# Strassen FFN kernel: late low parts, the down weight loads, the centre taps and one residual add change their places

## What is computed

```python
def conv_ffn(x, norm_g, w_up, conv_w, conv_b, w_down):      # w_up 1024 x 5632, w_down 2816 x 1024
    h = causal_depthwise_conv(rms_norm(x, norm_g) @ w_up, conv_w, conv_b)   # width 3
    g, u = jnp.split(h, 2, axis=-1)
    return (jax.nn.silu(g) * u) @ w_down

x = x + conv_ffn(x, ...)                                    # in both layers
z = rms_norm(x, norm_g) @ w_in                              # first step of layer 1's mixer
```

## Time and profile before

| | us |
|---|---|
| median of three runs | 2183.09 (2181.4 to 2183.55) |
| profiled execution | 2179.79 |
| its span, first to last instruction | 2178.0 |
| mean granted clock of TensorE | 0.991 |
| TensorE busy | 2117.4 |
| VectorE busy | 1419.3 |
| GpSimd busy | 1262.8 |
| ScalarE busy | 888.7 |

### The profile page before, as it was taken

How to read it: one execution, slowest core, us unless ns; L and a number is a source line. 1 busy time by engine, 2 the same in 40 slices (tenths; PEclk the granted TensorE clock), 3 DMA queues, 4 the chain that set the end, 5 groups by cost and what they waited for, 6 DMA issues and landing times. The chain is left out here.

```text
span 2178.0 us, 26915 instructions
## 1 busy us (share of the span) xinstructions
PE 2117.4 (97%) x10027; PEld 1741.1 (80%) x10027; DVE 1419.3 (65%) x1545; ACT 888.7 (41%) x1396; POOL 1262.8 (58%) x808
## 2 busy tenths in 40 slices
PE   9999999999999998998899999999999999999997
PEld 8777778878888787886788898888788788778876
DVE  7766777667777776565743344286777777765655
ACT  6555452544443433433344333434443344433331
POOL 2222117687778773688553333266877778745782
PEclk9999999999999999999999999999999999999999
DMA  6111003022232334343321021030222332333332
GB/s 204 58 49 40 34 17 139 21 87 87 92 131 91 113 107 182 108 134 108 131 88 49 30 72 54 30 136 29 78 81 94 116 116 87 119 145 135 139 130 87
DMA packets 57345, 204.19 MB, mean 94 GB/s; under 512 B 6848, under 2 KB 8960, under 8 KB 55168
## 3 DMA queue, kind: packets, MB, share of 16 engines
q1 hardware_dynamic: 47136, 163.22, 22.3%
q10 hardware_dynamic: 10080, 39.24, 4.9%
HBM read 151.81 MB, written 46.43 MB: 91 GB/s over the span
## 5 line engine op out<-in xcount | busy, mean ns | idle before, releaser
L1696 POOL TENSOR_TENSOR w_lo<-w_sum,w_hi 128x512 fp32r<-128x512 f32 x240 | 362.4, 1520 | 178.1 <-ACT w_hi L1690 178.1
L2318 POOL TENSOR_TENSOR w_hi<-w_raw,ones 128x1024 fp32r<-128x1024 f32 x54 | 106.3, 1969 | 496.1 <-PE pj L336 170.4
L1690 ACT ACTIVATE w_hi<-w_sum 128x512 fp32r<-128x512 f32 x240 | 145.3, 628 | 468.0 <-POOL w_sum L1711 194.7
L1696 POOL TENSOR_TENSOR w_lo<-w_raw,w_hi 128x512 fp32r<-128x512 f32 x180 | 240.5, 1344 | 90.4 <-ACT w_hi L1690 89.5
L1765 PE MATMUL pj<-t_hi,w_hi 128*128 128x512 f32 x520 | 205.5, 395 | 15.2 <-DVE ffn_v L1874 15.2
L1765 PE MATMUL pj<-t_lo,w_hi 128*128 128x512 f32 x520 | 203.7, 392 | 0.0
L1765 PE MATMUL pj<-t_hi,w_lo 128*128 128x512 f32 x520 | 203.5, 391 | 0.0
L1690 ACT ACTIVATE w_hi<-w_raw 128x512 fp32r<-128x512 f32 x180 | 111.6, 626 | 127.6 <-PE pj L1765 60.7
L1840 PE MATMUL dn<-pair,w_hi 128*128 128x512 f32 x512 | 158.2, 390 | 1.0 <-POOL w_lo L1696 0.9
L1840 PE MATMUL pj<-pair,w_hi 128*128 128x512 f32 x384 | 121.7, 399 | 18.2 <-POOL w_lo L1696 18.1
L2320 POOL TENSOR_TENSOR w_lo<-w_raw,w_hi 128x1024 fp32r<-128x1024 f32 x54 | 135.9, 2516 | 4.2
(11 more groups left out here) (421 smaller groups left out, 5449.5 us busy)
## 6 DMA issues: line engine op xcount, KB each, us to landing
w_raw<-weights SPq DMA_DIRECT2D x187, 512.0 KB, 3.9
gated_rows<-ffn_gated SPq DMA_DIRECT2D x72, 512.0 KB, 2.9
pair_stage<-gated_rows ACTq DMA_DIRECT2D x16, 1024.0 KB, 6.4
pair_stage<-gated_rows ACTq DMA_DIRECT2D x16, 512.0 KB, 4.5
x_first<-x_t SPq DMA_DIRECT2D x8, 512.0 KB, 7.4
res<-x_t SPq DMA_DIRECT2D x8, 512.0 KB, 6.5
pair_stage<-gated_rows ACTq DMA_DIRECT2D x16, 256.0 KB, 3.5
scratch<-res ACTq DMA_DIRECT2D x8, 512.0 KB, 2.7
```

Of the source, the lines that this page charges most:

```text
L1690: act.activation(f.cut(t, whi), f.source(j, name), ACT.Copy).then_inc(c_high, 1)
L1696: pool.tensor_tensor(f.cut(t, wlo), f.source(j, name), f.cut(t, whi).bitcast(F32), ALU.subtract).then_inc(c_ready, 1)
L2318: pool.tensor_tensor(whi[:, w, :], raw[:, r, :], ones[:, 0:1].to_broadcast([P, D]), ALU.mult).then_inc(w_high, 1)
```

## The change

Six places change, all in the order of work; no instruction is added or removed.

- DOWN_ORDER begins with chunk 20 (still in SBUF) and has chunk 0 second.
- In the last up tile VectorE makes the gated product of chunk 20 ahead of c11, and the first low part behind c11.
- `dve_gated_low` of the last two chunks moves from block 6 (ahead of the a22 and the s4 adds) to block 7 (behind u2, and behind the a11 add).
- SyncE issues the three weight loads of down ahead of the last pair's T transfers.
- On ScalarE `act_center(j - 1, 1)` stands ahead of the split of step 1, and `act_center(j, 0)` moves from behind the split of step 6 to ahead of that of step 4.
- `dve_layer1` goes add d, norm d - 1, for every d, where it had two adds and two norms, twice, and then add and norm in turn.

```diff
-DOWN_ORDER = (0, FC - 2, 1, 2, 3, FC - 1)
+DOWN_ORDER = (FC - 2, 0, 1, 2, 3, FC - 1)
...
             dve_block_add(dve, f, m, "u2", u, f.block_room("s2"))
+            if m == N_BLOCK - 1:
+                dve_gated_low(dve, f, DOWN_SIZES[0])
             dve_block_prod(dve, f, m, "s3")
...
             if m + 2 < N_PAIR:
                 dve_pair_low_half(dve, f, m + 2, 0)
-            elif m == N_BLOCK - 2:
-                dve_gated_low(dve, f, DOWN_SIZES[0])
             dve_block_prod(dve, f, m, "a22")
...
             if m + 2 < N_PAIR:
                 dve_pair_low_half(dve, f, m + 2, 1)
-            elif m == N_BLOCK - 2:
+            elif m == N_BLOCK - 1:
                 dve_gated_low(dve, f, DOWN_SIZES[0] + 1)
             dve_block_prod(dve, f, m, "s4")
...
             dve_c21(dve, f, j)
+            dve_gated(dve, f, j - 1)
+            dve_c11(dve, f, j)
             dve_gated_low(dve, f, 0)
-            dve_c11(dve, f, j)
-            dve_gated(dve, f, j - 1)
             dve_c12(dve, f, j)
...
                     if i == 1:
                         act_p1(act, f, j)
+                        if j > 1:
+                            act_center(act, f, j - 1, 1)
+                    if i == 4 and j < FC - 1:
+                        act_center(act, f, j, 0)
                     if t < N_PROD * FC:
                         act_cut(act, f, t)
...
                     if i == 0:
                         act_silu(act, f, j - 1)
-                    if i == 1 and j > 1:
-                        act_center(act, f, j - 1, 1)
-                    if i == 6:
-                        if j < FC - 1:
-                            act_center(act, f, j, 0)
...
             sp_gated_out(sp, f, FC - 3)
-            sp_pair_out(sp, f, N_PAIR - 1)
             for n in range(f.T1, f.T1 + 3):
                 sp_load(sp, n)
+            sp_pair_out(sp, f, N_PAIR - 1)
...
-            for two in ((0, 1), (2, 3), (4,), (5,), (6,), (7,)):
-                for d in two:
+            for d in range(KC + 1):
+                if d < KC:
                     dve_down(dve, f, LAST, d)
-                for d in two:
-                    dve.wait_ge(*down_final(f, d))
-                    dve_norm(dve, 2, d, XB, res[:, d, :])
+                if d:
+                    dve.wait_ge(*down_final(f, d - 1))
+                    dve_norm(dve, 2, d - 1, XB, res[:, d - 1, :])
```

## The result

| | before | after |
|---|---|---|
| median of the runs, us | 2182.7 (2181.4 to 2183.55, 4 runs) | 2128.81 (2127.13 to 2129.54, 4 runs) |
| profiled execution, us | 2179.79 | 2127.13 |
| its span, us | 2178.0 | 2125.3 |
| granted clock, mean | 0.991 | 1.000 |

The ratio is 0.9753 [0.9736, 0.9769]: 53.9 us less by the ratio, where the prediction had 50.5.

The account below looks back on a forecast made before the run. TensorE, busy for 97% of the span, was taken as the bound, so only its gaps and slow clock could pay. Gains of 14 + 18.5 + 5 + 13 = 50.5 us took the median from 2183.1 to 2132.6, say 2133; range 2126 to 2150.

Parts of the forecast that it names:

- 14 predicted: Start of the down projection: TensorE's wait for the first low part and slow matmuls behind it go, 14 of 14.4 us.
- 833.3: Start of down, layer 0: time in us when the second T transfer is issued, from which the first low part was timed.
- at nothing: SyncE's queue at the start of down: three weight loads passing ahead of the T transfers cost nothing.
- 2.3 + 1.7 us: First 48 matmuls of down: time lost to the slow clock, 2.3 us in layer 0 and 1.7 in layer 1.
- 18.5 predicted: Gap ahead of block 7: moving late low parts there removes two 8.3 us gaps and slow clock, 18.5 us net.
- 1.2 us a layer: Block 7: extra cost of two low parts on VectorE, taken as 1.2 us a layer, bounds 0 and 5.3.
- The third rival: Last block overflows: both low parts stretched, 5.3 us a layer plus slow clock, time 2145; chance 0.10.
- 5 predicted: First projection of layer 1: TensorE's 3.7 us wait on a residual add goes, with slow matmuls after it, 5 us.
- 13 predicted: Up tiles: earlier centre taps remove TensorE's waits on U3 sums, 13 of 15.2 us, bounds 0 and 15.2.
- 13.6 us: Up tiles: the ring holds five products, 13.6 us, ahead of need, so later splits were costed at nothing.
- The first rival: Up tiles: taps hold up splits, TensorE waits in all 42 tiles once lag passes 13.6 us; 2196, chance 0.03.
- Rivals 2 and 4: 2: T transfers late, Edit A worth nothing, 2147, chance 0.10. 4: VectorE's work keeps U3 late, Edit D nothing, 2146, 0.12.

Follow-up runs that it names:

- Edit A: Kernel before with only DOWN_ORDER, the order around chunk 20's gated product, and three weight loads ahead of the last T transfers changed: 2175.68 us, ratio 0.9961.
- Edit B: Kernel before with only the two late low parts moved from block 6 to block 7: 2166.76 us, ratio 0.9917.
- Edit C: Kernel before with only residual adds and norm parts taken in turn at the start of layer 1: 2178.59 us, ratio 0.9974.
- Edit D: Kernel before with only both centre taps moved ahead of the splits on ScalarE: 2164.59 us, ratio 0.991.

## Why the prediction was right, and where its steps were off

**Edit A, 14 predicted, 8.5 [5.9, 11.1] measured alone.** The mechanism was right, the size not. The chain from the T transfers' issue to the first low part's end was put at 840.5 - 833.3 = 7.2 us. It took 7.3: the two issues took 1.29 us, so the second stands at about 824.65, and the low part ended at 831.98. The landing, gated, high and low were each what was said. The step that failed is "833.3", taken as fixed against the end of the up products: the issue came 7.3 us ahead of that end in the kernel before, and only 6.3 (830.92 - 824.65) in the changed kernel. That 1 us is L1945, the T sum, 1.74 us instead of 0.68 because GpSimd's first down split now runs beside it. In layer 1 it is 2.18 for 0.68, and there the gap is 1.46. The prediction costed the moved loads on SyncE's queue "at nothing" and did not ask what else a load that lands earlier starts.

In the kernel with edit A alone 2.1 us of gaps are left in the two layers (0.57 + 1.49). A second part of the 14 did not come either, the slow matmuls. They were put at 2.3 + 1.7 us, the 48 matmuls of the first output chunk falling from 13.14 and 12.63 to 10.9. They take 11.66 in both layers: most of these 0.8 us are a wait for the second low part (chunk 0), stretched from 1.2 to 2.7 us beside GpSimd's second down split, so 1.6 of the 4 us stayed. Counted from the end of the up products to the first block, edit A alone gives 10.6 us in its profiled execution; from there to 8.5 is inside the interval.

The prediction was one step short a second time: it missed that the loads' landing is what lets ScalarE go on to the first high part, which was worth more than anything else in edit A (about 7 us in the kernel with the old queue). It saw the T values' wait and took the move for harmless when it was essential.

The Trainium skill, "SBUF — State Buffer", section "Who interferes with whom", says that the later of two such instructions waits for the whole of the earlier. This trace agrees to 0.2 us: in layer 1 of the kernel with edit A alone GpSimd ends at 1924.68 + 2.41 = 1927.09, and a T sum of 0.68 behind that would end at 1927.77; it ended at 1927.64. The prediction had weighed the rule for edit B, where it mattered less than in edit A.

**Edit B, 18.5 predicted, 18.1 measured.** Right in its place and its size. The extra cost in block 7 was put at 1.2 us a layer; by the waits in layer 0 of the changed kernel it is 0.88 + 0.52 - 0.74 = 0.66. The second low part took 2.25 us, stretched as the share adds were. The third rival, 5.3 us a layer, is refuted.

**Edit C, 5 predicted, 5.7 measured.** Right: 3.7 us of wait and the slow clock behind it.

**Edit D, 13 predicted, 19.7 [16.4, 22.7] measured.** The mechanism was right, two things in it were off. First the size, which lies above the upper bound of 15.2 that the prediction gave it. The term was the 15.2 us of U3 waits alone. The up projection from its first to its last matmul took 435.9 and 433.4 us before and 426.1 and 425.9 after, 17.3 us less, while its U3 waits fell by 12.9. Of the 4.4 us between them some 3.4 are matmuls at a lower clock behind one gap of 2.2 us in each layer (last section); the last 1 us was not taken apart. The prediction had added the clock to edits A, B and C, and not here, where the gaps were shorter. The profiled execution was also a mild one: the kernels that keep the old taps and change another part had U3 waits of 17.9, 18.8 and 15.3 us. Second, "so I cost the later splits at nothing". The sum stood, the reason did not. It named the ring's "13.6 us" ahead of need as the cover. With the hg tap alone the delay of the splits reached VectorE through the other tap, while no wait on a low split in the up tiles was among TensorE's, and with the tap two steps earlier such waits came, and a tile took 3.9 us longer. The later splits cost nothing here because the two taps move together. The first rival named a real mechanism and put its threshold in the wrong place; in this change it does not decide, since the U3 waits fell to 2.3 us and no waits on low splits appeared in the up tiles.

**Rivals 2 and 4** are refuted: A gives 8.5 us and not nothing, and D gives 19.7. VectorE's own work is not what kept U3 late.

**The sum, 50.5 predicted, 53.9 measured,** is closer than its terms: A was 5.5 too high, D 6.7 too low, and the two errors nearly cancel.

## What to carry to other kernels

When a step is moved on a queue, follow not only what it passes but what its earlier landing releases: here an early weight load freed the head of ScalarE's queue (a gain) and started a GpSimd split beside a VectorE sum (a loss). Where two engines hand work back and forth in order, test two moves together and apart before judging either; each alone may lose what both gain. A wait that the profile puts down to an engine is worth checking against the code when another instruction ended within 0.1 us of the resume.

## What the hardware showed that was not expected

A gap of 2.2 us was followed by a lower granted clock. The kernel before had such a gap on U3 that ended at 460.93 us. TensorE's row and the windows around it (columns as above):

```profile
460.93 0.47 PE L1765 MATMUL pj<-t_hi,w_hi 128*128 128x512 f32 x1 [2.23 <-DVE ffn_v L1874]
...
452.00:458.00 6.00, 6.00 (x28) 4.99 (x27) 4.64 (x4) 3.80 (x5) 4.85 (x5) 1.00 0.60 174
458.00:461.00 3.00, 0.77 (x5) 0.34 (x3) 2.86 (x5) 0.00 (x0) 2.87 (x3) 1.00 0.00 1
461.00:464.00 3.00, 3.00 (x9) 2.39 (x10) 1.51 (x2) 0.63 (x1) 2.20 (x3) 0.63 0.44 169
464.00:467.00 3.00, 3.00 (x12) 2.36 (x12) 1.43 (x2) 1.26 (x2) 2.20 (x3) 0.80 0.03 11
467.00:470.00 3.00, 3.00 (x15) 2.48 (x14) 1.49 (x2) 1.69 (x2) 2.94 (x2) 1.00 0.00 0
```

The two windows behind the gap hold 9 and 12 matmuls where 15 are usual: a mean between the 1.2 and the 2.4 GHz level. At 0.227 us each the 9 missing matmuls are 2.0 us; by the clock it is 3 x 0.37 + 3 x 0.20 = 1.7 us. Either is nearly the gap again. The changed kernel has no gap there:

```profile
461.00:464.00 3.00, 3.00 (x15) 2.49 (x14) 2.36 (x2) 0.63 (x1) 2.20 (x3) 1.00 0.22 86
```

Behind its gaps of 1.2 to 1.5 us at the start of down the mean clock stayed at 1.000. In between the outcome differs: in the kernel with the hg tap at step 2 a gap of 1.92 us that ended at 569.73 was followed by 4 us at a mean clock of 0.57, and one of 1.93 us that ended at 663.40 by 4 us at 1.00.
